# LayerNorm sums of a convolution branch: one ones-product per sum in chunks 1 to 3

## The chip, the cores and the metric

One core of one Trainium2 chip. The metric is the device time of one execution in microseconds; shown is the median of three runs.

## The reference

One layer of a streaming encoder for 2048 prompt frames and 64 sample frames. The convolution branch is the part that matters here: 512 channels, `u = a * sigmoid(gate)`, a causal depthwise convolution of width 31 plus a bias, then a LayerNorm over the 512 channels of each frame, swish, and a 512 x 512 projection `w_pw`.

```python
def _layernorm(x, g, b):
    mu = jnp.mean(xf, axis=-1, keepdims=True)
    xc = xf - mu
    y = xc * lax.rsqrt(jnp.mean(xc * xc, axis=-1, keepdims=True) + EPS)
    return y * g + b
...
c = _causal_dwconv(u_ext, w_dw) + b_dw
c = silu(_layernorm(c, g_cn, b_cn)) @ w_pw
```

The other branch is a stick-breaking attention of 8 heads. Both go through `w_out`, and a feed-forward layer (4096 wide, squared ReLU) follows.

## The kernel before

The frames are taken in four chunks of 512 (`NC = 4`); the last chunk carries the 64 sample frames as well. Every chunk passes through: gated projection (`ag`), k, v and q (`kvq`), convolution, LayerNorm, `pw`, attention, `out`, and the feed-forward layer. A product with a weight is made of three products of high and low parts (`mm3`: lines 2282 to 2284).

The order is written by hand, in slots. `window(c)` runs the feed-forward layer of chunk c in slots on every engine and, inside the same slots, the LayerNorm, `pw` and attention of chunk n = c + 1. A round `e` has 16 slots in windows 0 to 2: positions 0 to 7 are halves of f1 products (group j ends in the odd position 2j + 1), positions 8 to 15 are f2 products; a slot is twelve matrix products. After an f1 group ScalarE does ReLU, square and the high part (lines 1699, 1701, 1710), then VectorE writes `hid_lo` (line 2199). After an f2 product VectorE adds to `resid` (line 2189). In a slot each engine goes through its list in a fixed order: on VectorE weight splits (line 1787), convolution taps, the LayerNorm's step, `pw`'s low part, attention, f2's adds, `hid_lo`; on TensorE the LayerNorm's step, `pw`, then the slot's twelve products, then attention.

The LayerNorm of chunk c begins at slot `ln0(c)` of the window: 22, 18 and 14 for chunks 1, 2 and 3. The channels lie on partitions in four blocks (`CB = 4`) of 128, so a sum over channels is a product with a matrix of ones. Before the change, `ln` went by steps, one per slot:

- step 0, TensorE: four ones-products into one PSUM bank, the sum over channels (line 2440)
- step 1, VectorE: subtracts the mean from the four blocks (line 1979); ScalarE: their squares into `csq` (line 1520)
- step 2, TensorE: four ones-products over `csq` (line 2447)
- step 3, VectorE: variance (line 1983); ScalarE: Ln and Exp (lines 1523, 1525)
- step 4 on: VectorE refines the inverse root (lines 1986 to 1991) and scales, ScalarE and POOL make the sigmoid and the affine part, VectorE multiplies, `cT_hi` (ScalarE, line 1544) and `cT_lo` (VectorE, line 2007) follow, the last in step 11

Chunk 3 has a second piece of 64 columns (the sample), whose steps run 8 slots later. Chunk 0 has its LayerNorm in `front`.

`pw_slot(c)` is `ln0(c) + LN_STEPS` (8 more in chunk 3): 34, 30, 34. From there `pw`'s four products stand in four slots, each at the head of its slot; their results go out over ScalarE and VectorE (lines 1553, 2015) and SP (line 1058). Attention begins at `att_first(c) = pw_slot(c) + 4 + 1` and ends at slot 116; its steps are spread evenly over the slots between.

The weights pass through a ring of eight slabs in the order of `weight_order`; SP loads slab n when slab n - 8 is freed (`load_slab`, lines 844 to 865). `pw`'s two slabs have their place in that order by `pw_slot`:

```python
for e in range(FFE):
    w += [("f1", c, 4 * e + j) for j in range(4)]
    if pw and e == pw_slot(c + 1) // 16:
        w += pw
    w += [("f2", c, 4 * e + j) for j in range(4)]
```

Of the kernel before, what the change touches and what calls it, by code (L numbers as in the profile page):

```python
# [7 lines left out]
ALU = mybir.AluOpType  # L8
# [9 lines left out]
CC, CW = 512, 31  # L18
CB = CC // P
# [5 lines left out]
NC = SEQ // CHUNK  # L25
# [22 lines left out]
def conv_pieces(c):  # L48
    return [(0, 0, CHUNK)] + ([(SMP, CHUNK, DEC)] if c == NC - 1 else [])
# [72 lines left out]
    return 8 + 2 * len(tiles(c))  # L122


LN_STEPS = 12

EARLY = 11
LATE = [20, 43, 36, 28]
# [6 lines left out]
def ln0(c):  # L135

    return (LATE[c] + 1) // 2


def pw_slot(c):  # L140

    return ln0(c) + LN_STEPS + (8 if c == NC - 1 else 0)


def pw_step(c):
# [184 lines left out]
def build(nc, x_prompt, x_sample, cache_k, cache_v, state_conv, g_mix, w_in, w_dw, b_dw, g_cn, b_cn, w_pw,  # L330
# [3 lines left out]
    with ctx:  # L334
# [29 lines left out]
        ones = place("ones", [P, P])  # L364
# [32 lines left out]
        for c in range(2):  # L397
            n = TMAX if c else CHUNK
# [99 lines left out]
        def sem(name):  # L498
            return ctx.enter_context(nc.semaphore(name))
# [18 lines left out]
        kq_st = [sem(f"kq_st{i}") for i in range(2)]  # L518
        vp_out = [sem(f"vp_out{i}") for i in range(2)]
        sd_ok, id_ok = sem("sd_ok"), sem("id_ok")  # L520
        mean_ps, xc_ok, sq_ok, var_ps, var_ok, lnr_ok, yn_ok, sg_ok, cm_ok, c_hi, c_lo, cvo_ps, cvo_ok, cvo_out = (
            sem(n) for n in ("mean_ps", "xc_ok", "sq_ok", "var_ps", "var_ok", "lnr_ok", "yn_ok", "sg_ok", "cm_ok",
                             "c_hi", "c_lo", "cvo_ps", "cvo_ok", "cvo_out"))
        pw_ps, pw_hi, pw_lo, out_ps, out_add = (sem(n) for n in ("pw_ps", "pw_hi", "pw_lo", "out_ps", "out_add"))
        pw_st = [sem(f"pw_st{i}") for i in range(2)]
# [285 lines left out]

        def ln_step(c, slot):

            return [(n, slot - ln0(c) - 8 * n) for n in range(len(conv_pieces(c))) if 0 <= slot - ln0(c) - 8 * n < LN_STEPS]

        block = ctx.enter_context(nc.Block())

# [386 lines left out]
        def _(pool):  # L1204
# [40 lines left out]
            def ln(c, n, step):  # L1245
                a, q0, w = conv_pieces(c)[n]
                lb = c + n
                k = step - 5
                if 0 <= k < CB:
                    pool.wait_ge(yn_ok, CB * lb + k + 1)  # L1250
                    if CB * lb + k >= 2:
                        pool.wait_ge(cm_ok, CB * lb + k - 1)
                    nc.gpsimd.tensor_scalar(cid[:, k % 2, 0:w], conv_sum(c, k, a, w), vecs[:, k, CW + 1:CW + 2],
                                            vecs[:, k, CW + 2:CW + 3], ALU.mult, ALU.add).then_inc(id_ok, 1)
# [87 lines left out]
        def _(act):  # L1342
# [168 lines left out]
            def ln(c, n, step):  # L1511
                a, q0, w = conv_pieces(c)[n]
                lb = c + n
                nt = len(tiles(c))
                if step == 1:
                    if n:
                        act.wait_ge(yn_ok, CB * lb)
                    for k in range(CB):
                        act.wait_ge(xc_ok, CB * lb + k + 1)
                        nc.scalar.activation(csq[:, k, 0:w], conv_sum(c, k, a, w), ACT.Square).then_inc(sq_ok, 1)  # L1520
                if step == 3:
                    act.wait_ge(var_ok, lb + 1)
                    nc.scalar.activation(lnr[:, 0:w], lnv[:, 0:w], ACT.Ln).then_inc(sd_ok, 1)
                    act.wait_ge(sd_ok, 2 * lb + 1)
                    nc.scalar.activation(lnr[:, 0:w], lnr[:, 0:w], ACT.Exp, scale=-0.5).then_inc(sd_ok, 1)
                    nc.scalar.activation(unused[:], ident[:, 0:1], ACT.Sigmoid)
                k = step - 5
                if 0 <= k < CB:
                    act.wait_ge(yn_ok, CB * lb + k + 1)
                    if CB * lb + k >= 2:  # L1530
                        act.wait_ge(cm_ok, CB * lb + k - 1)
                    nc.scalar.activation(csig[:, k % 2, 0:w], conv_sum(c, k, a, w), ACT.Sigmoid,
                                         bias=vecs[:, k, CW + 2:CW + 3], scale=vecs[:, k, CW + 1:CW + 2]).then_inc(sg_ok, 1)
                if step == 7 and n == 0:
                    for m in (2 * nt - 2, 2 * nt - 1):
                        act.wait_ge(kq_st[m % 2], kq_stores(c, m))
                    for i in (nt - 2, nt - 1):
                        act.wait_ge(*value_stored(c, i))
                    act.wait_ge(vo_out[0], 16 * (2 * c + (nt + 1) // 2))
                    act.wait_ge(vo_out[1], 16 * (2 * c + 2))  # L1540
                k = step - 7
                if 0 <= k < CB:
                    act.wait_ge(cm_ok, CB * lb + k + 1)
                    nc.scalar.copy(cT_hi[:, k, a:a + w], conv_sum(c, k, a, w)).then_inc(c_hi, 1)
# [235 lines left out]
        def _(dve):  # L1780
# [192 lines left out]
            def ln(c, n, step):  # L1973
                a, q0, w = conv_pieces(c)[n]
                lb = c + n
                if step == 1:
                    dve.wait_ge(mean_ps, lb + 1)
                    for k in range(CB):
                        nc.vector.scalar_tensor_tensor(out=conv_sum(c, k, a, w), in0=ps[:, Z_BANK, 0:w], scalar=-1.0 / CC,
                                                       in1=conv_sum(c, k, a, w), op0=ALU.mult, op1=ALU.add).then_inc(xc_ok, 1)  # L1980
                if step == 3:
                    dve.wait_ge(var_ps, lb + 1)
                    nc.vector.tensor_scalar(lnv[:, 0:w], ps[:, Z_BANK + 1, 0:w], 1.0 / CC, EPS, ALU.mult, ALU.add).then_inc(var_ok, 1)
                if step == 4:
                    dve.wait_ge(sd_ok, 2 * lb + 2)
                    nc.vector.scalar_tensor_tensor(out=ntmp[:, 0:w], in0=lnr[:, 0:w], scalar=-0.5, in1=lnr[:, 0:w],
                                                   op0=ALU.mult, op1=ALU.mult).then_inc(lnr_ok, 1)
                    dve.wait_ge(lnr_ok, 3 * lb + 1)
                    nc.vector.tensor_tensor(ntmp[:, 0:w], ntmp[:, 0:w], lnv[:, 0:w], ALU.mult).then_inc(lnr_ok, 1)
                    dve.wait_ge(lnr_ok, 3 * lb + 2)  # L1990
                    nc.vector.scalar_tensor_tensor(out=lnr[:, 0:w], in0=ntmp[:, 0:w], scalar=1.5, in1=lnr[:, 0:w],
                                                   op0=ALU.add, op1=ALU.mult).then_inc(lnr_ok, 1)
                    dve.wait_ge(lnr_ok, 3 * lb + 3)
                    dve.wait_ge(xc_ok, CB * (lb + 1))
                for k in {4: (0,), 5: (1, 2), 6: (3,)}.get(step, ()):
                    nc.vector.tensor_tensor(conv_sum(c, k, a, w), conv_sum(c, k, a, w), lnr[:, 0:w],
                                            ALU.mult).then_inc(yn_ok, 1)
                k = step - 6
                if 0 <= k < CB:
                    dve.wait_ge(sg_ok, CB * lb + k + 1)  # L2000
                    dve.wait_ge(id_ok, CB * lb + k + 1)
                    nc.vector.tensor_tensor(conv_sum(c, k, a, w), csig[:, k % 2, 0:w], cid[:, k % 2, 0:w],
                                            ALU.mult).then_inc(cm_ok, 1)
                k = step - 8
                if 0 <= k < CB:
                    dve.wait_ge(c_hi, CB * lb + k + 1)
                    nc.vector.tensor_tensor(conv_low(c, k, a, w), conv_sum(c, k, a, w),
                                            cT_hi[:, k, a:a + w].bitcast(F32), ALU.subtract).then_inc(c_lo, 1)
# [271 lines left out]
        def _(pe):  # L2280
# [151 lines left out]
            def ln(c, n, step):  # L2432
                a, q0, w = conv_pieces(c)[n]
                lb = c + n
                if step == 0:
                    if n:
                        pe.wait_ge(xc_ok, CB * lb)
                    for k in range(CB):
                        pe.wait_ge(taps, TAPS * c + taps_in_order[c].index((k, CW - 1)) + 1)
                        ins = nc.tensor.matmul(ps[:, Z_BANK, 0:w], ones[:], conv_sum(c, k, a, w), start=k == 0, stop=k == CB - 1)  # L2440
                    ins.then_inc(mean_ps, 1)
                if step == 2:
                    if n:
# [312 lines left out]
```

## Time and profile before

| | before |
|---|---|
| median of 3 runs | 2761.16 us (2758.79 to 2766.84) |
| profiled execution | 2764.65 us, its span 2762.8 us |
| TensorE, weight loads of TensorE | 96%, 81% of the span |
| VectorE, ScalarE, POOL | 65%, 41%, 21% |
| mean granted clock of TensorE | 0.989 of full speed |

A busy share is an average over the whole span. What a step costs has to be read in its own stretch: from the timeline of each engine there, in which a bracket at the end of a row gives the idle time before the instruction and the one that ended it.

### The profile page before, as it was taken

The numbers are of one execution on the slowest core, as the hardware profiler recorded it, in microseconds if no ns is written. First come the engines' busy times: TensorE is split into PE (matmuls) and PEld (weight loads), VectorE is DVE, ScalarE is ACT, GpSimd is POOL, SyncE is SP. The second block draws the span as 40 slices with busy tenths as digits, with TensorE's granted clock in tenths as the row PEclk, the third lists the DMA queues.
The fourth block names the chain that finished last, engine by engine and source line by source line (L and its number), as shares of the span: only waits on it lengthen the run. The fifth ranks groups of instructions, "written<-read, shape, count | busy, mean of one in ns | idle before, by whom it ended". The sixth has DMA issues, their size and how long they took to land. (4 is left out here: it accounts for less than half of the span.)

```text
span 2762.8 us, 37728 instructions
## 1 busy us (share of the span) xinstructions
PE 2665.8 (96%) x13832; PEld 2248.4 (81%) x13832; DVE 1782.7 (65%) x2776; ACT 1123.7 (41%) x2221; POOL 580.8 (21%) x523
## 2 busy tenths in 40 slices
PE   7988899999999999999999999999999999999999
PEld 6757778788887888788888797778888887889998
DVE  6996777577762577367775358736888851755444
ACT  4334524455552122355554212334666630333342
POOL 2122210022210010032231002102333310434230
PEclk9999999999999999999999999999999999999999
DMA  9796797697669568465554746854455447355452
GB/s 325 254 342 205 234 353 276 254 332 264 254 219 370 220 220 288 168 232 181 182 179 156 308 183 220 266 203 148 151 191 174 163 160 293 122 187 179 167 198 96
DMA packets 294754, 616.21 MB, mean 223 GB/s; under 512 B 23665, under 2 KB 188529, under 8 KB 250029
## 3 DMA queue, kind: packets, MB, share of 16 engines
q1 hardware_dynamic: 294573, 613.80, 62.7%
q8 instruction: 113, 1.85, 0.3%
q14 instruction: 68, 0.56, 0.1%
HBM read 444.79 MB, written 168.94 MB: 222 GB/s over the span
## 5 line engine op out<-in xcount | busy, mean ns | idle before, releaser
L1265 POOL TENSOR_TENSOR beta<-beta,stay 128x512 f32<-128x512 f32 (+3 forms) x328 | 312.4, 953 | 890.1 <-DVE stay L2035 854.1
L2282 PE MATMUL ps<-h2T_hi,w_s 128*128 128x512 f32 (+2 forms) x976 | 370.7, 380 | 8.4 <-DMA w_s<-w_scratch 4.4
L2284 PE MATMUL ps<-h2T_hi,w_s 128*128 128x512 f32 (+2 forms) x976 | 359.2, 368 | 0.0
L2283 PE MATMUL ps<-h2T_lo,w_s 128*128 128x512 f32 (+2 forms) x976 | 358.9, 368 | 0.0
L1569 ACT ACTIVATE stay<-ps 128x512 f32<-128x512 f32 (+3 forms) x328 | 174.7, 533 | 346.5 <-PE ps L2483 223.8
L2550 PE MATMUL ps<-w_s,hid_hi 128*128 128x512 f32 x768 | 308.3, 401 | 0.0
L2551 PE MATMUL ps<-w_s,hid_lo 128*128 128x512 f32 x768 | 299.9, 390 | 0.0
L2552 PE MATMUL ps<-w_s,hid_hi 128*128 128x512 f32 x768 | 299.8, 390 | 0.0
L2189 DVE TENSOR_TENSOR resid<-ps,resid 128x512 f32<-128x512 f32 x256 | 174.0, 686 | 192.5 <-PE ps L2552 191.8
L2035 DVE TENSOR_TENSOR_SCAN stay<-stay,stay,ones 128x512 f32<-128x512 f32 x192 | 274.3, 1429 | 0.0
L1827 DVE SCALAR_TENSOR_TENSOR cacc<-uT,vecs,cacc 128x512 f32<-128x512 f32 (+1 forms) x360 | 259.6, 776 | 1.5
L2199 DVE TENSOR_TENSOR hid_lo<-ps,hid_hi 128x512 fp32r<-128x512 f32 x96 | 66.2, 690 | 261.9 <-ACT hid_hi L1710 261.9
L2282 PEld LDWEIGHTS ps<-h2T_hi,w_s 128*128 128x128 f32 x976 | 185.2, 190 | 38.4 <-DMA w_s<-w_scratch 4.5
L2284 PEld LDWEIGHTS ps<-h2T_hi,w_s 128*128 128x128 f32 x976 | 184.8, 189 | 30.9
L2283 PEld LDWEIGHTS ps<-h2T_lo,w_s 128*128 128x128 f32 x976 | 185.4, 190 | 26.3 <-issue 1.0
L2045 DVE TENSOR_TENSOR aT_lo<-ps,aT_hi 128x512 fp32r<-128x512 f32 (+3 forms) x328 | 189.5, 578 | 14.6 <-ACT aT_hi L1581 8.6
L2483 PE MATMUL ps<-a_k,a_q 128*128 128x512 f32 (+3 forms) x640 | 186.7, 370 | 8.8 <-DMA a_k<-k_scratch 8.3
L1581 ACT CAST aT_hi<-ps 128x512 fp32r<-128x512 f32 (+3 forms) x328 | 174.3, 531 | 19.3 <-PE ps L2493 14.7
L2493 PE MATMUL ps<-ident,beta 128*128 128x128 f32 (+1 forms) x1104 | 174.9, 273 | 7.2 <-DVE aT_lo L2045 7.0
L1570 ACT ACTIVATE beta<-ps 128x512 f32<-128x512 f32 (+3 forms) x328 | 173.7, 530 | 0.0
L2552 PEld LDWEIGHTS ps<-w_s,hid_hi 128*128 128x128 f32 x768 | 144.2, 188 | 31.9
L2550 PEld LDWEIGHTS ps<-w_s,hid_hi 128*128 128x128 f32 x768 | 144.4, 188 | 28.5 <-DVE resid L2189 0.4
(267 smaller groups left out, 5840.7 us busy)
## 6 DMA issues: line engine op xcount, KB each, us to landing
w_s<-w_scratch SPq DMA_DIRECT2D x254, 1024.0 KB, 8.3
w_scratch<-w_s SPq DMA_DIRECT2D x94, 1024.0 KB, 8.6
w_raw<-in_w_ff SPq DMA_DIRECT2D x92, 512.0 KB, 5.6
a_k<-k_scratch SPq DMA_DIRECT2D x80, 256.0 KB, 3.8
a_v<-v_scratch SPq DMA_DIRECT2D x80, 256.0 KB, 4.1
a_q<-q_scratch SPq DMA_DIRECT2D x64, 256.0 KB, 4.7
w_s<-w_scratch SPq DMA_DIRECT2D x28, 512.0 KB, 6.5
w_raw<-in_w_in SPq DMA_DIRECT2D x20, 512.0 KB, 7.9
```

Source lines behind the costliest of these rows:

```text
L1265: nc.gpsimd.tensor_tensor(v[0:q.r, 0:n], v[0:q.r, 0:n], stay_of(q.z)[0:q.r, 1:n + 1], ALU.mult).then_inc(s_a, 1)
L1827: nc.vector.scalar_tensor_tensor(out=acc, in0=uT[:, k, tap:tap + wd], scalar=vecs[:, k, tap:tap + 1], in1=acc, op0=ALU.mult, op1=ALU.add). ...
L2035: nc.vector.tensor_tensor_scan(v[0:q.r, 0:q.n][:, ::-1], v[0:q.r, 0:q.n][:, ::-1], ones[0:q.r, 0:1].to_broadcast([q.r, q.n]), init, ALU.mu ...
L2045: ins = nc.vector.tensor_tensor(aT_lo[:, o, 0:full, q.t * P:q.t * P + q.r], bank[:, 0:full * q.r].rearrange("p (a b) -> p a b", a=full), a ...
L2282: nc.tensor.matmul(out, w[0], x[0], start=start, stop=False)
L2283: nc.tensor.matmul(out, w[0], x[1], start=False, stop=False)
L2284: return nc.tensor.matmul(out, w[1], x[0], start=False, stop=stop)
L2483: ins = nc.tensor.matmul(ps[0:q.r, Z_BANK + q.z % 2, 0:q.n], x, a_k[:, k0:k0 + q.n], start=v == 0, stop=v == 1)
L2493: ins = nc.tensor.transpose(ps[0:w, T_BANK + q.z % 2, b * q.r:(b + 1) * q.r], beta[q.z % 4][0:q.r, b * P:b * P + w], ident[0:q.r, 0:q.r])
L2550: nc.tensor.matmul(o, hid_hi[x][:, k, q0:q0 + r], wh[:, c0:c0 + BANK], start=k == 0, stop=False)
L2551: nc.tensor.matmul(o, hid_lo[x][:, k, q0:q0 + r], wh[:, c0:c0 + BANK], start=False, stop=False)
L2552: ins = nc.tensor.matmul(o, hid_hi[x][:, k, q0:q0 + r], wl[:, c0:c0 + BANK], start=False, stop=k == 3)
```

## The change

In chunks 1 to 3, VectorE adds the four blocks up to one before each sum (two adds, then one that waits for both), and TensorE makes one ones-product of the result. The adds take a step each: step 0 the fold of the sums, step 1 the product, step 2 the subtractions and squares, step 3 the fold of the squares, step 4 the product; everything after it comes two steps later. So the LayerNorm has 14 steps in these chunks, not 12, and `pw_slot` is 36, 32, 36; `att_first` moves with it. `csq` holds the folds. Chunk 0 stays as it is. ScalarE's, POOL's and the later VectorE steps are the same with `later = 2` added to their step.

```diff
-LN_STEPS = 12
+def ln_steps(c):
+    return 14 if c else 12
...
-    return ln0(c) + LN_STEPS + (8 if c == NC - 1 else 0)
+    return ln0(c) + ln_steps(c) + (8 if c == NC - 1 else 0)
...
             def ln(c, n, step):
                 a, q0, w = conv_pieces(c)[n]
                 lb = c + n
-                if step == 1:
+                later = 2 if c else 0
+                if c and step == 0:
+                    if c == 1:
+                        dve.wait_ge(out_ps, 8)
+                    dve.wait_ge(kvq_ps, 12 * c + 3 * len(tiles(c)))
+                    if n:
+                        dve.wait_ge(yn_ok, CB * lb)
+                    for h in range(2):
+                        for k in (2 * h, 2 * h + 1):
+                            dve.wait_ge(taps, TAPS * c + taps_in_order[c].index((k, CW - 1)) + 1)
+                        nc.vector.tensor_tensor(csq[:, h, 0:w], conv_sum(c, 2 * h, a, w), conv_sum(c, 2 * h + 1, a, w),
+                                                ALU.add).then_inc(folded, 1)
+                    dve.wait_ge(folded, 6 * (lb - 1) + 2)
+                    nc.vector.tensor_tensor(csq[:, 0, 0:w], csq[:, 0, 0:w], csq[:, 1, 0:w], ALU.add).then_inc(folded, 1)
+                if c and step == 3:
+                    for h in range(2):
+                        dve.wait_ge(sq_ok, CB * lb + 2 * h + 2)
+                        nc.vector.tensor_tensor(csq[:, 2 * h, 0:w], csq[:, 2 * h, 0:w], csq[:, 2 * h + 1, 0:w],
+                                                ALU.add).then_inc(folded, 1)
+                    dve.wait_ge(folded, 6 * (lb - 1) + 5)
+                    nc.vector.tensor_tensor(csq[:, 0, 0:w], csq[:, 0, 0:w], csq[:, 2, 0:w], ALU.add).then_inc(folded, 1)
+                if step == (2 if c else 1):
                     dve.wait_ge(mean_ps, lb + 1)
...
-                if step == 0:
+                if c and step == 1:
                     if n:
                         pe.wait_ge(xc_ok, CB * lb)
+                    pe.wait_ge(folded, 6 * (lb - 1) + 3)
+                    nc.tensor.matmul(ps[:, Z_BANK, 0:w], ones[:], csq[:, 0, 0:w], start=True, stop=True).then_inc(mean_ps, 1)
+                if c and step == 4:
+                    if n:
+                        pe.wait_ge(var_ok, lb)
+                    pe.wait_ge(folded, 6 * (lb - 1) + 6)
+                    nc.tensor.matmul(ps[:, Z_BANK + 1, 0:w], ones[:], csq[:, 0, 0:w], start=True, stop=True).then_inc(var_ps, 1)
+                if c == 0 and step == 0:
...
```

## Rows read from the trace of the kernel before

**Rows 1.** The page, first part: busy time, share of the span, instructions.

```profile
PE 2665.8 (96%) x13832; PEld 2248.4 (81%) x13832; DVE 1782.7 (65%) x2776; ACT 1123.7 (41%) x2221; POOL 580.8 (21%) x523
```

**Rows 2.** Waits of TensorE, whole span: waited for, total us, times, longest.

```profile
PE ps L2282 <- DMA w_s<-w_scratch: 5.5, 3, 4.4
```

**Rows 3.** Timeline of TensorE, chunks 1 and 3: start, us, instruction, idle before.

```profile
484.26 1.02 PE L2440 MATMUL ps<-cacc_second,ones 128*128 128x512 f32 x2
486.87 2.84 PE L2440 MATMUL ps<-cacc_second,ones 128*128 128x512 f32 x6 [1.58 <-DVE cacc_second L1827]
489.15 0.80 PE L2282 MATMUL ps<-h2T_hi,w_s 128*128 128x512 f32 x1
...
495.02 3.60 PE L2447 MATMUL ps<-csq,ones 128*128 128x512 f32 x8
498.05 0.79 PE L2550 MATMUL ps<-w_s,hid_hi 128*128 128x512 f32 x1
498.68 0.39 PE L2551 MATMUL ps<-w_s,hid_lo 128*128 128x512 f32 x1
...
1810.06 1.00 PE L2440 MATMUL ps<-cacc,ones 128*128 128x64 f32 x8
1810.87 0.47 PE L2282 MATMUL ps<-h2T_hi,w_s 128*128 128x512 f32 x1
```

**Rows 4.** Timeline of VectorE, chunk 1's LayerNorm.

```profile
488.06 0.68 DVE L2199 TENSOR_TENSOR hid_lo<-ps,hid_hi 128x512 fp32r<-128x512 f32 x1
488.66 1.21 DVE L1787 TENSOR_TENSOR w_s<-w_raw,w_s 128x1024 fp32r<-128x1024 f32 x1
489.80 2.47 DVE L1979 SCALAR_TENSOR_TENSOR cacc_second<-ps,cacc_second 128x512 f32<-128x512 f32 x4
497.06 0.69 DVE L2199 TENSOR_TENSOR hid_lo<-ps,hid_hi 128x512 fp32r<-128x512 f32 x1 [4.79 <-ACT hid_hi L1710]
...
505.88 0.68 DVE L1986 SCALAR_TENSOR_TENSOR ntmp<-lnr 128x512 f32<-128x512 f32 x1
506.60 0.69 DVE L1989 TENSOR_TENSOR ntmp<-ntmp,lnv 128x512 f32<-128x512 f32 x1
```

**Rows 5.** Timeline of ScalarE, chunk 1's squares and chunk 3's `cvout`.

```profile
490.51 2.43 ACT L1520 ACTIVATE csq<-cacc_second 128x512 f32<-128x512 f32 x4 [3.29 <-DVE cacc_second L1979]
...
1804.52 1.04 ACT L1682 COPY cvout<-ps 30x512 f32<-30x512 f32 x2
```

**Rows 6.** Timelines of TensorE and VectorE, chunks 2 and 3.

```profile
1096.22 3.60 PE L2440 MATMUL ps<-cacc,ones 128*128 128x512 f32 x8
...
1098.26 0.69 DVE L2199 TENSOR_TENSOR hid_lo<-ps,hid_hi 128x512 fp32r<-128x512 f32 x1 [3.58 <-ACT hid_hi L1710]
...
1780.60 0.69 DVE L2189 TENSOR_TENSOR resid<-ps,resid 128x512 f32<-128x512 f32 x1 [0.39 <-PE ps L2552]
...
1812.36 0.69 DVE L2199 TENSOR_TENSOR hid_lo<-ps,hid_hi 128x512 fp32r<-128x512 f32 x1 [2.56 <-ACT hid_hi L1710]
```

**Rows 7.** Timeline of TensorE: waits for weight slabs, chunks 2 and 3.

```profile
1168.89 0.80 PE L2282 MATMUL ps<-h2T_hi,w_s 128*128 128x512 f32 x1 [4.38 <-DMA w_s<-w_scratch]
1174.08 0.40 PE L2483 MATMUL ps<-a_k,a_q 128*128 128x256 f32 x2
...
1839.15 0.39 PE L2282 MATMUL ps<-h2T_hi,w_s 128*128 128x512 f32 x1
...
1846.67 0.47 PE L2282 MATMUL ps<-cT_hi,w_s 128*128 128x512 f32 x1 [0.54 <-DMA w_s<-w_scratch]
```

**Rows 8.** TensorE's timeline, and stretches: length, busy by engine, granted clock, DMA.

```profile
178.22 1.13 PE L2440 MATMUL ps<-cacc,ones 128*128 128x512 f32 x2 [1.90 <-DVE cacc L1827]
178.00:181.00 3.00, 2.78 (x10) 1.99 (x11) 2.62 (x6) 0.81 (x2) 0.00 (x0) 1.00 1.08 282
...
1862.42 0.50 PE L2282 MATMUL ps<-cT_hi,w_s 128*128 128x512 f32 x1 [3.23 <-DVE pwo L2015]
1863.00:1867.00 4.00, 4.00 (x13) 3.13 (x12) 0.00 (x0) 0.00 (x0) 0.00 (x0) 0.57 0.49 180
```

More of the change, by code:

```diff
@@ L520, in build @@
         sd_ok, id_ok = sem("sd_ok"), sem("id_ok")
-        mean_ps, xc_ok, sq_ok, var_ps, var_ok, lnr_ok, yn_ok, sg_ok, cm_ok, c_hi, c_lo, cvo_ps, cvo_ok, cvo_out = (
-            sem(n) for n in ("mean_ps", "xc_ok", "sq_ok", "var_ps", "var_ok", "lnr_ok", "yn_ok", "sg_ok", "cm_ok",
+        folded, mean_ps, xc_ok, sq_ok, var_ps, var_ok, lnr_ok, yn_ok, sg_ok, cm_ok, c_hi, c_lo, cvo_ps, cvo_ok, cvo_out = (
+            sem(n) for n in ("folded", "mean_ps", "xc_ok", "sq_ok", "var_ps", "var_ok", "lnr_ok", "yn_ok", "sg_ok", "cm_ok",
                              "c_hi", "c_lo", "cvo_ps", "cvo_ok", "cvo_out"))
@@ L812, in ln_step @@
         def ln_step(c, slot):
-            return [(n, slot - ln0(c) - 8 * n) for n in range(len(conv_pieces(c))) if 0 <= slot - ln0(c) - 8 * n < LN_STEPS]
+            return [(n, slot - ln0(c) - 8 * n) for n in range(len(conv_pieces(c))) if 0 <= slot - ln0(c) - 8 * n < ln_steps(c)]
         block = ctx.enter_context(nc.Block())
@@ L1247, in ln @@
                 lb = c + n
-                k = step - 5
+                k = step - 5 - (2 if c else 0)
                 if 0 <= k < CB:
@@ L1520, in ln @@
                         nc.scalar.activation(csq[:, k, 0:w], conv_sum(c, k, a, w), ACT.Square).then_inc(sq_ok, 1)
-                if step == 3:
+                if step == 3 + later:
                     act.wait_ge(var_ok, lb + 1)
@@ L1526, in ln @@
                     nc.scalar.activation(unused[:], ident[:, 0:1], ACT.Sigmoid)
-                k = step - 5
+                k = step - 5 - later
                 if 0 <= k < CB:
@@ L1533, in ln @@
                                          bias=vecs[:, k, CW + 2:CW + 3], scale=vecs[:, k, CW + 1:CW + 2]).then_inc(sg_ok, 1)
-                if step == 7 and n == 0:
+                if step == 7 + later and n == 0:
                     for m in (2 * nt - 2, 2 * nt - 1):
@@ L1540, in ln @@
                     act.wait_ge(vo_out[1], 16 * (2 * c + 2))
-                k = step - 7
+                k = step - 7 - later
                 if 0 <= k < CB:
@@ L1975, in ln @@
                 lb = c + n
-                if step == 1:
+                later = 2 if c else 0
+                if c and step == 0:
[18 more added lines that the diff above has]
+                    nc.vector.tensor_tensor(csq[:, 0, 0:w], csq[:, 0, 0:w], csq[:, 2, 0:w], ALU.add).then_inc(folded, 1)
+                if step == (2 if c else 1):
                     dve.wait_ge(mean_ps, lb + 1)
@@ L1980, in ln @@
                                                        in1=conv_sum(c, k, a, w), op0=ALU.mult, op1=ALU.add).then_inc(xc_ok, 1)
-                if step == 3:
+                if step == 3 + later:
                     dve.wait_ge(var_ps, lb + 1)
                     nc.vector.tensor_scalar(lnv[:, 0:w], ps[:, Z_BANK + 1, 0:w], 1.0 / CC, EPS, ALU.mult, ALU.add).then_inc(var_ok, 1)
-                if step == 4:
+                if step == 4 + later:
                     dve.wait_ge(sd_ok, 2 * lb + 2)
@@ L1994, in ln @@
                     dve.wait_ge(xc_ok, CB * (lb + 1))
-                for k in {4: (0,), 5: (1, 2), 6: (3,)}.get(step, ()):
+                for k in {4: (0,), 5: (1, 2), 6: (3,)}.get(step - later, ()):
                     nc.vector.tensor_tensor(conv_sum(c, k, a, w), conv_sum(c, k, a, w), lnr[:, 0:w],
                                             ALU.mult).then_inc(yn_ok, 1)
-                k = step - 6
+                k = step - 6 - later
                 if 0 <= k < CB:
@@ L2003, in ln @@
                                             ALU.mult).then_inc(cm_ok, 1)
-                k = step - 8
+                k = step - 8 - later
                 if 0 <= k < CB:
@@ L2441, in ln @@
                     ins.then_inc(mean_ps, 1)
-                if step == 2:
-                    if n:
-                        pe.wait_ge(var_ok, lb)
+                if c == 0 and step == 2:
                     for k in range(CB):
```

## The prediction

> **What bounds the kernel now.** I read the page first, then the waits of TensorE, then its timeline around the ones-products of chunks 1 to 3, then VectorE and ScalarE in the same stretches, and last the granted clock. TensorE is busy for 96% of the span [rows 1]: what it no longer does, or no longer waits for, counts in full, and so does a new wait. Around the change a window slot is twelve products; 24 products run from 489.15 to 495.02 [rows 3], so with 0.40 for the slow first one a product takes 0.228 us and a slot 2.74. VectorE and ScalarE follow one slot behind, with slack that differs from slot to slot: after the second half of an f1 product, VectorE must wait for three ScalarE passes before it can write `hid_lo`. The product that ended at 495.02 [rows 3] got its `hid_lo` at 497.06 [rows 4]: 2.05 us, and VectorE is free at 2.65. That distance decides this case.
>
> **What is removed.** A ones-product appears as two passes. The four of chunk 1's variance hold TensorE from 495.02; the next product starts at 498.05, the one after it at 498.68 instead of 498.28 [rows 3]. So eight passes cost 3.43 us and six of them 2.57. Six sums of 512 columns (a mean and a variance in each of three chunks): 15.4. The 64-column sums of chunk 3's second piece cost 0.81 for eight passes (1810.06 to 1810.87) [rows 3], so six cost 0.6; two sums: 1.2. Chunk 1's wait of 1.58 for the last taps [rows 3] goes: 1.6. TensorE waits three times for a weight slab from the scratch, 5.5 in all with a longest of 4.4 [rows 2]. The two short ones (1.1 together) are chunk 1's and 3's first `pw` products; their slabs now have two more slots to land. The long one stands in chunk 2 at 1168.89 [rows 7]: f1 slabs 10 and 11 take ring places that `pw` frees. There `pw_slot` goes from 30 to 32, `feed_forward_order` divides it by 16, and so chunk 2's `pw` slabs move from e = 1 to e = 2 and those f1 slabs no longer stand behind them. That gives 4.38, and the half-speed stretch after it: twelve products took 5.19 (1168.89 to 1174.08 [rows 7]) instead of 2.74, thus 2.45. Together 6.8. Removed: 15.4 + 1.2 + 1.6 + 1.1 + 6.8 = 26.1.
>
> **What is added on VectorE.** A fold is two independent adds and one that waits for them. Independent operations of 512 columns follow each other at 0.60 (four in 2.47), dependent ones at 0.72 (505.88 to 506.60) [rows 4]; a fold takes 2.0 and reaches TensorE 0.1 later. VectorE's 65% [rows 1] does not make it free: each fold has its place in the queue.
>
> Chunk 1, mean. Without the products TensorE ends slot 22 at 484.26 + 2.74 = 487.0 [rows 3]. VectorE writes slot 21's `hid_lo` at 488.06 and a weight split until 489.87 [rows 4]; the fold is ready at 491.9. Wait 4.9.
> Chunk 1, variance. Let E be the end of slot 23, an f1 half: `hid_lo` done for the queue at E + 2.65, a split 1.15, four subtractions 2.47, the last square 0.67 after them (ScalarE ends at 492.94 [rows 5], VectorE at 492.27 [rows 4]), then one add and the dependent one: ready at E + 8.5. TensorE arrives two slots after E, at 5.5. Wait 3.0. Before, the subtractions fell behind slot 22, which has no `hid_lo`: moving them by one slot is what loses the slack.
> Chunk 2, mean. TensorE would end slot 18 at 1096.22 + 2.74 = 1098.96; `hid_lo` of slot 17 starts at 1098.26 [rows 6], so the fold is ready at 1101.0: wait 2.0. Variance: as in chunk 1 but no split, E + 7.45 against 5.46: wait 2.0.
> Chunk 3, first piece. Slots 13 and 15 end in f2 adds, which need no ScalarE: the add at 1780.60 [rows 6] starts right behind slot 13's product, 0.6 later the fold can start, and 0.6 + 2.0 + 0.1 = 2.7 is just the length of the slot that TensorE has to do. The same holds one step on for the variance. I take 0.1 for each.
> Chunk 3, second piece, mean. TensorE is now early: it began slot 22 at 1810.06 [rows 3], less 4.9 (two sums saved, 0.2 waited), and with 2.74 for the slot it reaches slot 23 at 1807.9. The fold stands behind slot 21's `hid_lo`, which was at 1812.36 [rows 6]. That moves up less, to about 1808.9: the root now sits at slot 19, where ScalarE also has the copies of `cvout` (1.04 [rows 5]) ahead of the gate of that slot, and the first sigmoid ahead of that of slot 21. Two more 512-column operations and a small fold follow: 0.6 + 0.6 + 0.6 for what is queued and 0.6 for the fold with its latency, ready at 1811.3, wait 3.4. Variance, from E as above: 2.65, four operations of 512 columns 2.4, four small subtractions 0.6 and the small fold with its latency 0.65 make E + 6.3 against 5.5: wait 0.8.
> Waits in all: 4.9 + 3.0 + 2.0 + 2.0 + 0.2 + 3.4 + 0.8 = 16.3.
>
> **The clock.** The granted clock falls after some waits. After 3.23 us at 1862.42 it is 0.57 on average over 4 us, a mix of its full level (2.4 GHz) and its half (1.2); after 1.90 at 178.22 it stays at 1.00 [rows 8]. At 0.57 for 4 us the toll is 4 x 0.43 = 1.7. I charge it for 4.9, 3.0 and 3.4, not for the two waits of 2.0, which lie nearer to 1.90: 5.1. The bounds: 0 (none falls) and 5 x 2.45 = 12.3 (all five fall, at the toll of rows 7). The Trainium skill, page "TensorE: Matmul & The Clock Gate", Part 1, states that the number of products run cold varies from run to run with the phase of the monitor; the two tolls seen here, 1.7 and 2.45, fit, and by it the sum would keep its middle and only spread.
>
> **What moves.** Chunk 2's `pw` slabs now go into places that f2 of e = 1 frees at the end of slot 31, and the first `pw` product stands at the head of slot 32, with no slot between. Nothing else is in SP's queue before them in that slot. In chunk 3 the same slabs are released at 1839.15, and the second is there at 1846.67 [rows 7]: 7.5. TensorE can do six products (1.37) as soon as the first lands, so 6.1 is lost, plus a clock toll that lies partly under the second transfer: 0.9. Together 7.0. Bounds: 6.1 (no toll) and 8.6 (6.1 + 2.45).
> The rest of the LayerNorm (Ln, Exp, POOL's scale-and-shift, sigmoids, `cT_lo`) moves two slots together with `pw`, so the number of slots between its last step and `pw` stays, and the first `pw` product has no wait for `cT_lo` to take over. SP's stores of `pwo` move with it and the attention's loads a little. Attention starts two slots later and ends at the same slot 116: chunk 3's 154 steps fall into 75 slots, not 77, so four slots get three steps. TensorE does the same work; I take 0, with 2 us as the upper bound (a wait of about 0.5 in each of the four). If `pwo`'s wait of 3.23 in chunk 3 [rows 8] goes with the later start, that is a gain of up to 4.9; it hangs on slot parity, which stays, so 0. SP, POOL and ScalarE issue the same number of instructions; VectorE gets 24 more, under its waits for TensorE elsewhere.
>
> **Sum.** 16.3 + 5.1 + 7.0 - 26.1 = +2.3. The profiled execution took 2764.65, 3.5 above the median of the three runs; against the median: 2761.16 + 2.3 = 2763.5.
>
> **The rivals.**
> A, the folds come in time. If VectorE runs ahead of where I put it, the 16.3 of waits and their 5.1 of clock go: 2763.5 - 21.4 = 2742.1. For it: VectorE is idle for 35% of the span [rows 1]. Against it: the `hid_lo` rows stand directly ahead of the fold's place in chunks 1 and 2, and ScalarE's three passes cannot be shortened. A half of it, with chunk 1's split out of the way and chunk 3's second piece in time, saves about half of that: some 2752. Chance 0.13.
> B, the clock, on the other side. Place: behind the five waits of 2.0 and more, and behind chunk 2's slab wait. Price: 2.45 each, not 1.7 thrice, is 12.3 - 5.1 = 7.2, and 1.6 more at the slabs: 2763.5 + 8.8 = 2772.3. It decides once these six stretches cost 2.0 each, 12.0 instead of the 6.0 charged. For it: [rows 7]; against it: [rows 8], the clock held after 1.90 us. Chance 0.15.
>
> **How the numbers follow.** About 0.3% (8.3 us) is what a measurement of this kernel can tell from no change. The forecast with its bounds (clock 0 to 12.3, slabs 6.1 to 8.6, attention 0 to 2, each seldom at its end) gives 2756 to 2770; its chance is 0.72. The range reaches to A's half and most of the way to B: 2752 to 2771. Faster by over 0.3% is A (0.13), slower is B (0.15), within is the forecast (0.72).
>
> **What would show it.** In the profile of the changed kernel each 512-column sum is one product of two passes. The waits of TensorE should name the folds on VectorE, the longest of some 5 us in chunk 1, 2 and 2 in chunk 2, and about 3.4 in chunk 3's second piece; the clock should be below 1.0 after the long ones. In chunk 2 there should be a wait of 5 to 6 us for the slabs of `pw` at the head of slot 32, and none at slot 36. I am wrong if the folds show no waits (A), if `pw` in chunk 2 starts at once, or if attention takes visibly longer.

## The result and the profile after

| | before | after |
|---|---|---|
| median, 5 runs of each on one chip | 2761.16 us (2758.79 to 2767.27) | 2773.43 us (2769.49 to 2778.66) |
| ratio with 95% interval | | 1.0044 [1.0034, 1.0055] |
| profiled execution, its span | 2764.65, 2762.8 us | 2773.43, 2771.6 us |

The change makes the kernel slower by 12.3 us. The forecast was 2763.5, with a range of 2752 to 2771. Between the two profiled executions the difference is 8.8, because the one of before lay 3.5 above its median; the stages below add up to those 8.8.

First line of the page, after: busy time, share of the span and instructions. It answers to [rows 1].

```profile
PE 2658.5 (96%) x13784; PEld 2243.4 (81%) x13784; DVE 1802.6 (65%) x2800; ACT 1122.0 (40%) x2221; POOL 590.7 (21%) x523
```

TensorE has 48 instructions fewer and is busy 7.3 us less; VectorE has the 24 more that were counted. With less to do and a span 8.8 longer, TensorE must stand still for some 16 us more. The waits of TensorE over the whole span, after (engine, line, waited for: us in total, times, longest):

```profile
PE ps L2522 <- DVE aT_lo L2068: 16.3, 23, 2.3
...
PE ps L2462 <- DVE csq L1991: 9.7, 3, 4.7
...
PE ps L2467 <- DVE csq L1998: 5.2, 3, 2.8
PE ps L2305 <- DMA w_s<-w_scratch: 4.9, 1, 4.9
```

The two `csq` lines are the folds and the `w_scratch` line is the slab wait; both were forecast. The top line is the attention, and it was not: in before the same wait is

```profile
PE ps L2493 <- DVE aT_lo L2045: 7.0, 16, 0.9
```

The folds one by one, in TensorE's timeline after (start, us, instruction, idle time before it); they answer to [rows 3], the `pw` rows to [rows 7, 8]:

```profile
489.75 2.08 PE L2462 MATMUL ps<-csq,ones 128*128 128x512 f32 x2 [4.72 <-DVE csq L1991]
...
503.49 2.07 PE L2467 MATMUL ps<-csq,ones 128*128 128x512 f32 x2 [2.83 <-DVE csq L1998]
...
1098.41 1.12 PE L2462 MATMUL ps<-csq,ones 128*128 128x512 f32 x2 [1.83 <-DVE csq L1991]
...
1109.43 1.12 PE L2467 MATMUL ps<-csq,ones 128*128 128x512 f32 x2 [1.69 <-DVE csq L1998]
...
1142.66 0.77 PE L2305 MATMUL ps<-cT_hi,w_s 128*128 128x512 f32 x1 [4.88 <-DMA w_s<-w_scratch]
...
1812.88 0.41 PE L2462 MATMUL ps<-csq,ones 128*128 128x64 f32 x2 [3.12 <-DVE csq L1991]
...
1823.86 0.41 PE L2467 MATMUL ps<-csq,ones 128*128 128x64 f32 x2 [0.72 <-DVE csq L1998]
...
1868.46 0.69 PE L2305 MATMUL ps<-cT_hi,w_s 128*128 128x512 f32 x1 [3.22 <-DVE pwo L2038]
```

Each sum is one product of two passes. The first wait is long for the reason given ahead of the run, as VectorE's timeline after shows; its fold is the last two rows:

```profile
485.96 0.68 DVE L2222 TENSOR_TENSOR hid_lo<-ps,hid_hi 128x512 fp32r<-128x512 f32 x1
486.56 1.21 DVE L1789 TENSOR_TENSOR w_s<-w_raw,w_s 128x1024 fp32r<-128x1024 f32 x1
487.69 1.28 DVE L1988 TENSOR_TENSOR csq<-cacc_second,cacc_second 128x512 f32<-128x512 f32 x2
489.01 0.69 DVE L1991 TENSOR_TENSOR csq<-csq 128x512 f32<-128x512 f32 x1
```

VectorE is never idle here: `hid_lo` and a weight split of 1.21 stand ahead of the fold while TensorE waits. The clock behind these waits (stretch, its length, busy by engine, granted clock, DMA share, GB/s), answering to [rows 8]:

```profile
490.00:494.00 4.00, 4.00 (x10) 2.50 (x11) 0.00 (x0) 0.00 (x0) 0.00 (x0) 0.62 1.03 368
503.50:507.50 4.00, 4.00 (x9) 2.54 (x10) 2.27 (x3) 2.32 (x2) 0.00 (x0) 0.60 1.03 425
1098.40:1101.40 3.00, 2.99 (x11) 2.17 (x12) 0.00 (x0) 0.00 (x0) 0.00 (x0) 1.00 1.02 429
1109.40:1112.40 3.00, 2.97 (x11) 2.16 (x12) 1.38 (x2) 2.60 (x4) 0.00 (x0) 1.00 1.06 376
1142.60:1146.60 4.00, 3.94 (x9) 3.04 (x10) 0.00 (x0) 0.00 (x0) 0.00 (x0) 0.50 1.01 426
1813.00:1817.00 4.00, 4.00 (x13) 3.19 (x14) 0.76 (x1) 0.62 (x2) 0.99 (x2) 0.62 0.01 2
```

In this execution it falls behind the waits of 4.72, 2.83, 4.88 and 3.12 and stays at 1.00 behind those of 1.83 and 1.69. The last section shows that the 1.83 does not always leave it there.

**Where the 8.8 us are.** TensorE's timeline was cut in both profiles at the first `out` product, the first `kvq` product, the first `pw` product and the first score of each chunk. The LayerNorm's stage has two more slots in it after the change and the attention's two fewer; they are taken out at 2.74 each (5.48). The forecast's terms are put beside them:

| stage | forecast | measured |
|---|---|---|
| chunk 1, up to `pw` | +4.6 | +2.9 |
| chunk 1, `pw` | -0.6 | -1.6 |
| chunk 1, attention | 0 | -2.7 |
| chunk 2, up to `pw`, without the slab wait | -1.1 | -1.0 |
| chunk 2, slab wait and `pw` | +7.0 | +4.9 + 2.7 |
| chunk 2, attention: the old slab wait and its toll | -6.8 | -6.8 |
| chunk 2, the rest of the attention | 0 | +3.1 |
| chunk 3, up to `pw` | -0.2 | -0.4 |
| chunk 3, `pw` | -0.6 | -0.8 |
| chunk 3, attention | 0 | +8.3 |
| everything else | 0 | +0.2 |
| sum | +2.3 | +8.8 |

(In chunk 2's attention only the sum of its two lines, -3.7, is measured; the old wait and its toll are [rows 7].) One line is far off: chunk 3's attention. To see it in the profile, take three rounds of 16 slots each, cut where VectorE writes the `hid_lo` of slots 49, 65, 81 and 97. Before:

```profile
1936.20:2022.70 86.50, 85.24 (x494) 72.74 (x493) 73.71 (x116) 55.36 (x117) 32.19 (x32) 1.00 0.50 163
2022.70:2109.20 86.50, 85.28 (x494) 72.79 (x493) 73.71 (x116) 55.43 (x118) 32.19 (x32) 1.00 0.50 167
2109.20:2195.80 86.60, 85.34 (x494) 72.85 (x493) 73.75 (x117) 55.46 (x118) 32.20 (x32) 1.00 0.49 160
```

After:

```profile
1930.70:2020.43 89.73, 87.49 (x508) 74.38 (x507) 75.02 (x119) 56.11 (x120) 32.70 (x33) 1.00 0.48 157
2020.43:2111.56 91.13, 86.64 (x500) 73.56 (x500) 76.27 (x118) 56.26 (x120) 35.84 (x33) 1.00 0.47 156
2111.56:2198.42 86.86, 85.87 (x493) 72.41 (x491) 74.92 (x116) 55.09 (x117) 32.27 (x32) 1.00 0.48 164
```

Before, every round is the same 86.5. After, the first two last 89.7 and 91.1 and the third is back at 86.9, all at a full clock. The first two hold 33 steps of attention and not 32, which is about (86.5 - 16 x 2.74)/32 = 1.3 us of the difference in each, moved there from elsewhere; the rest is lost. In the second, TensorE is idle for 91.13 - 86.64 = 4.5, against 1.2 before.

What differs between the rounds is how the steps are dealt. Before, 154 steps fall on 77 slots, 39 to 115: each slot has steps 2i and 2i + 1, an even pair. After, 75 slots share them, and three steps fall in slots 59, 78, 97 and 115. Behind a slot with three, the pairs are shifted: slots 60 to 77 and 98 to 114 hold the second step of one old pair and the first of the next, an odd pair, and slots 79 to 96 hold even pairs again. The second round above is mostly odd (12 of its 16 slots), and its 4.5 of waits stand in the odd slots 68, 70 and 72; the third is nearly all even. From 1884 to 2318, before:

```profile
PE ps L2493 <- DVE aT_lo L2045: 5.1, 12, 0.6
```

and after, the same stretch:

```profile
PE ps L2522 <- DVE aT_lo L2068: 11.5, 14, 2.3
```

So the profile names 6.4 of the 8.3. Counted by slot, TensorE's waits in chunk 3's attention after, all causes together, are 6.7 in the 35 odd slots, 2.8 in the four with three steps (2.33 of it in slot 97) and 2.3 in the 36 even ones; before, the 77 even slots have 5.8.

### The profile page after: what moved, and what is told of

It is laid out like the page before. It is cut to its first block and busy times, and to the rows that moved or that the text cites. A ratio compares the mean times of both kernels' runs of the same rounds, so it can differ in the third digit from the quotient of the medians.

```text
span 2771.6 us, 37664 instructions
## 1 busy us (share of the span) xinstructions
PE 2658.5 (96%) x13784; PEld 2243.4 (81%) x13784; DVE 1802.6 (65%) x2800; ACT 1122.0 (40%) x2221; POOL 590.7 (21%) x523
## 3 DMA queue, kind: packets, MB, share of 16 engines
q8 instruction: 113, 1.85, 0.3%
## 5 line engine op out<-in xcount | busy, mean ns | idle before, releaser
L2522 PE MATMUL ps<-ident,beta 128*128 128x128 f32 (+1 forms) x1104 | 175.1, 274 | 16.7 <-DVE aT_lo L2068 16.3
L2522 PEld LDWEIGHTS ps<-ident,beta 128*128 128x128 f32 (+1 forms) x1104 | 132.7, 140 | 54.2 <-issue 28.4
L2581 PEld LDWEIGHTS ps<-w_s,hid_hi 128*128 128x128 f32 x768 | 144.4, 188 | 31.8
```

The source lines that it names most:

```text
L2522: ins = nc.tensor.transpose(ps[0:w, T_BANK + q.z % 2, b * q.r:(b + 1) * q.r], beta[q.z % 4][0:q.r, b * P:b * P + w], ident[0:q.r, 0:q.r])
L2581: ins = nc.tensor.matmul(o, hid_hi[x][:, k, q0:q0 + r], wl[:, c0:c0 + BANK], start=False, stop=k == 3)
```

## The experiments

All ratios are against the kernel before, run beside it on the same chip; "after" is the changed kernel of the section above. Three questions were open: whether the attention's loss comes from its later start, what the folds and the slab stall are worth alone, and then whether the three-step slots or the shifted pairs cost the time.

**1. The attention ends two slots later (e1).** The changed kernel, attention ending at slot 118 in chunks 1 to 3, so that it has as many slots as before again (77 in chunks 1 and 3, 81 in chunk 2).

```diff
-    return 58 if c == 0 else 116
+    return 58 if c == 0 else 118
```

> The changed kernel (2773.4), with the attention of chunks 1 to 3 ending at slot 118, not 116, so that it has as many slots as before the change: chunk 3 has two steps in each of 77 slots again. Theory 1, the attention's denser steps cost the time: in chunk 3 the stretch from the first score to the output projection is 426.5 us, against 423.7 less two slots of 2.74 before, so 8.3 too long, with 11.5 us of waits for aT_lo against 5.1; in chunk 2 some 3 us. Both go: 2762 to 2765, the waits for aT_lo in chunk 3 back at about 5. Rival, the loss is in the LayerNorm's folds and the clock after them (and the attention only shows it): within 2 us of 2773.

Measured: 2772.24, ratio 1.0046 [1.0033, 1.0058]: no gain in all, as the rival had it. But the stages of the theory moved as it said: chunk 3's attention took 8.9 less than after, chunk 2's 3.1 less. Chunk 1's took 9.5 more, and TensorE's timeline there has a wait that neither kernel had:

```profile
805.12 0.79 PE L2512 MATMUL ps<-a_k,a_q 128*128 128x512 f32 x1 [5.36 <-DMA a_k<-k_scratch]
```

Chunk 1's slots decide when loads of `a_k` can start. The expectation missed that, and experiment 5 leaves chunk 1 alone.

**2. The kernel before, with the later start alone (e2).**

```diff
-    return pw_slot(c) + pw_step(c) * CB + 1
+    return pw_slot(c) + pw_step(c) * CB + (3 if c else 1)
```

> The kernel before (2761.2) with nothing of the change but the later start of attention: two slots later in chunks 1 to 3, the end stays at slot 116. No fold, 12 steps, slabs as before. Theory 1 (denser steps): 2769 to 2773, slower by 8 to 11, with waits for aT_lo of 2 us in chunk 3. Rival (folds and clock): within 2 us of 2761.

Measured: 2768.81, ratio 1.0028 [1.0016, 1.0039]. No fold, no moved slab, and a loss of about 7. From 1884 to 2318 its wait is that of after, to the digit:

```profile
PE ps L2493 <- DVE aT_lo L2045: 11.5, 14, 2.3
```

The later start with the old end is enough to make this loss. Chunk 3's attention is 429.46 long here, 2.9 more than after with the same waits, because the clock fell behind two of them (1.85 and 2.33) that left it at full in the profiled execution after.

**3. Chunk 2's `pw` slabs earlier (e3).** The changed kernel, with these slabs put between f2 of e = 1 and f1 of e = 2.

```diff
-        if pw and e == pw_slot(c + 1) // 16:
+        if pw and c != 1 and e == pw_slot(c + 1) // 16:
             w += pw
         w += [("f2", c, 4 * e + j) for j in range(4)]
+        if pw and c == 1 and e == 1:
+            w += pw
```

> The changed kernel (2773.4) with chunk 2's two pw slabs in another place of the weight order, between f2 of e = 1 and f1 of e = 2: they then take ring places that f1 of e = 1 frees, some twelve slots before their use. Theory 1: this removes the wait of 4.9 at the head of slot 32 and the half-speed stretch behind it (2.7), so 2765 to 2767, and leaves the waits for aT_lo in chunks 2 and 3 as they are. Rival, the slab wait hides work that VectorE has to do anyway: the wait moves to the pw results or the attention's first steps and less than 3 us is gained.

Measured: 2764.76, ratio 1.0012 [1.0003, 1.0020], 8.7 under after. The wait of 4.88 is gone; the stages up to `pw` and of `pw` are 5.0 and 2.7 shorter than after. So the stall cost 7.7, of which 2.7 lay behind the wait itself, not the 0.9 of the forecast.

**4. Both (e4).** Edits 1 and 3 together.

> Both edits, attention to slot 118 and chunk 2's slabs early. Theory 1, the two costs lie in different stretches and add up: 2773.4 - 9.5 - 7.6 = 2754 to 2758, faster than the kernel before. If the two overlap: no better than the better one alone.

Measured: 2765.05, ratio 1.0014 [1.0005, 1.0023]. A miss: chunk 1's attention lost 9.6 to `a_k`, as in e1, which cancels the gain elsewhere.

**5. The later end in chunks 2 and 3 only (g1).**

```diff
-    return 58 if c == 0 else 116
+    return 58 if c == 0 else 116 if c == 1 else 118
```

> The changed kernel (2773.4) with the attention of chunks 2 and 3 alone ending at slot 118; chunk 1's ends at 116 as in the changed kernel. Theory 1 in its second form: the first try took 8.9 us out of chunk 3's attention and 3.1 out of chunk 2's, and gave 9.5 back in chunk 1, where the shifted steps ran into a 5.4 us wait for a_k. Without chunk 1: 2760 to 2763. Rival (a fixed sum of time that shows up wherever the trace has room): again about 2772.

Measured: 2760.44, ratio 0.9997 [0.9989, 1.0006], 13.0 under after. Its wait from 1884 to 2318:

```profile
PE ps L2522 <- DVE aT_lo L2068: 5.6, 13, 0.7
```

That is before's again (5.1, 12, 0.6). By stage it gains 8.7 in chunk 3's attention and 3.1 in chunk 2's, 11.8 together.

**6. The changed order without the folds (g6).** Four ones-products per sum, in steps 1 and 4; everything else as after. The core of it, next to the folds' removal on VectorE:

```diff
-                if c and step == 1:
+                if step == (1 if c else 0):
...
-                if c == 0 and step == 2:
+                if step == (4 if c else 2):
```

> The changed kernel (2773.4) without the folds: the schedule with its 14 steps, pw and attention two slots later and the slab order stay, but TensorE makes four ones-products again in steps 1 and 4 and VectorE adds nothing up. Theory: the folds save 15.4 + 1.2 of products and cost 14.9 of waits and three stretches of slow clock, 4.6 by the granted clock after them, so the folds alone are worth nothing: 2768 to 2774, with the waits for csq gone and no low clock in chunk 1's LayerNorm. Rival 1, the folds are the loss: 2761. Rival 2, the folds gain what the removed products cost: 2785 to 2790.

Measured: 2765.43, ratio 1.0019 [1.0011, 1.0028], 8.0 under after. It was expected that the folds would be worth about nothing; they cost. How much is less sure: the profiled execution here is the fastest of its twelve, 3.5 below their median, and by the two ratios the difference is 6.9, give or take some 4. By stage, after against this kernel, the stretches that hold the folds give chunk 1 +5.7, chunk 2 -1.2 and chunk 3 -0.3, together 4.2. The `pw` stages give another +1.0 in chunk 2 and +1.6 in chunk 3, but those hold no fold: both kernels have the same waits there (4.9 and 3.2), and behind them the clock was 0.50 and 0.57 over 4 us after, 0.57 and 1.00 here. Chunk 1's thirty microseconds without folds (stretch, length, TensorE's busy time first, the granted clock third from the end):

```profile
480.00:510.00 30.00, 30.00 (x120) 22.09 (x119) 16.84 (x23) 13.55 (x18) 0.00 (x0) 1.00 0.94 345
```

and with them, after:

```profile
480.00:510.00 30.00, 22.45 (x81) 16.34 (x80) 19.24 (x26) 10.14 (x14) 0.00 (x0) 0.89 0.90 332
```

7.55 us of waits and a clock of 0.89, to save two sums of 2.57. In chunk 2, where the waits are short and the clock held in this execution, the folds win 1.2; where it fell behind the first of them, as in g1, the same stage is 1.7 longer and the gain is gone. This kernel also shows that chunk 1's tap wait of 1.58 [rows 3] went through the later slot, not through the fold.

**7. Edits 3 and 5 together (g2).**

> Chunk 2's slabs early and the attention of chunks 2 and 3 to slot 118. Theory: both gains in full, 2773.4 - 8.7 - 12 = 2752 to 2755, faster than the kernel before by 0.25 to 0.35%. If they overlap: 2760.

Measured: 2753.54, ratio 0.9973 [0.9962, 0.9984]: faster than before. The gain is 19.9 where 8.7 and 13.0 make 21.7: the two losses are separate and add up, within the noise.

**8. The LayerNorm of chunks 1 and 2 one slot later (g8).** On top of g2, so that a fold no longer stands right behind a `hid_lo`. Shown against the changed kernel, without edit 3.

```diff
-    return (LATE[c] + 1) // 2
+    return (LATE[c] + 1) // 2 + (1 if c in (1, 2) else 0)
...
-    return 58 if c == 0 else 116
+    return 58 if c == 0 else (116, 119, 118)[c - 1]
```

> The kernel just named, and the LayerNorm of chunks 1 and 2 begins one slot later (23 and 19), so that the folds and subtractions follow slots without hid_lo; chunk 2's attention ends at 119. Theory, the waits come from the slot parity: chunk 1's 4.7 falls to about 2, its 2.8 and chunk 2's 1.8 and 1.7 vanish, with the slow clock behind them; 8 us less than the kernel just named, 2744 to 2748. Rival, VectorE is simply late there: the waits stay within 1 us of what they were, 2752 to 2755.

Measured: 2745.41 (2743.34 to 2748.97), ratio 0.9947 [0.9935, 0.9958]: faster than both kernels, by 15.9 and 28. The folds' waits in TensorE's timeline:

```profile
486.33 1.88 PE L2464 MATMUL ps<-csq,ones 128*128 128x512 f32 x2 [2.01 <-DVE csq L1993]
...
498.40 1.13 PE L2469 MATMUL ps<-csq,ones 128*128 128x512 f32 x2 [1.13 <-DVE csq L2000]
...
1102.08 1.13 PE L2469 MATMUL ps<-csq,ones 128*128 128x512 f32 x2 [1.83 <-DVE csq L2000]
```

Chunk 1's went from 4.72 and 2.83 to 2.01 and 1.13, and chunk 2's first is gone. Chunk 2's second, expected to vanish, is 1.83 (1.69 after): one slot later it is this fold that stands right behind a `hid_lo`, in VectorE's timeline:

```profile
1099.41 0.69 DVE L2224 TENSOR_TENSOR hid_lo<-ps,hid_hi 128x512 fp32r<-128x512 f32 x1 [3.25 <-ACT hid_hi L1714]
1100.02 1.28 DVE L1997 TENSOR_TENSOR csq<-csq 128x512 f32<-128x512 f32 x2
```

Both the waits that went and the one that stayed fit the forecast's account, that a fold's price is its place in VectorE's queue behind `hid_lo`. That the folds pay in this kernel is not shown: no run has its deal and slabs without the folds, and g2's 2753.5 less what the folds cost (4 to 8 by g6) would be near the same time.

**9. The kernel before with odd pairs (h1).** Chunk 3's steps shifted by one: one step in slot 39, odd pairs in 40 to 115, the last step in 116. No slot has three steps. This and the next tell the two theories of the attention's loss apart.

```diff
-    if slot < a or slot >= b:
+    if slot < a or slot >= b + (c == NC - 1):
         return range(0)
+    if c == NC - 1:
+        return range(max(0, 2 * (slot - a) - 1), min(n, 2 * (slot - a) + 1))
```

> The kernel before (2761.3), where each slot of chunk 3's attention holds an even step and the next odd one; here all of chunk 3's steps move by one, so that slot 39 holds one step, slots 40 to 115 an odd step and the next even one, and slot 116 the last. No slot has three steps, and nothing else changes. Theory 2, the pairing: in the changed kernel slots 65 to 80, nearly all with odd pairs, took 91.1 us (33 steps) against 86.5 (32 steps) with even pairs; over 76 slots that is some 15 to 20 us, 2775 to 2781. Theory 1, the slots with three steps: 2760 to 2763.

Measured: 2774.26, ratio 1.0038 [1.0026, 1.0051], just under the expected 2775. Chunk 3's attention took 10.8 more than before. Its wait from 1884 to 2318:

```profile
PE ps L2495 <- DVE aT_lo L2047: 13.3, 20, 1.1
```

The theory of the three-step slots foretold no loss here. It falls as the whole cause: odd pairs lose time without any such slot.

**10. The changed kernel with even pairs (h2).** The same 75 slots; slots 78 and 115 take four steps, all the others one old pair.

```diff
+    if c == NC - 1:
+        return range(2 * (n // 2 * (slot - a) // (b - a)), 2 * (n // 2 * (slot - a + 1) // (b - a)))
```

> The changed kernel (2773.4), attention of chunk 3 still in slots 41 to 115, but its steps are dealt out in whole even pairs: two slots (78 and 115) hold four steps, all others two. Theory 2, the pairing: chunk 3's stretch falls from 426.5 to 418 to 420 us, in all 2765 to 2767. Theory 1, the slots with more than two steps: no better than 2771.

Measured: 2766.70, ratio 1.0015 [1.0006, 1.0024], 6.7 under after. Chunk 3's attention is 420.06 long against 426.52, and the wait from 1884 to 2318 falls back:

```profile
PE ps L2524 <- DVE aT_lo L2070: 5.6, 11, 1.2
```

Against before's 418.2 (423.67 less the two slots), 1.9 are left. That is what two fewer slots cost with the pairs kept (the two slots of four steps have 1.3 of waits). The other 6.5 of the 8.3 go with the odd pairs and the slots of three steps, which this edit takes out together.

**11. The kernel before with the earlier slabs (f1).** Edit 3 on before, where it should remove the wait of 4.38 [rows 7].

> The kernel before (2761.3) with nothing of the change but chunk 2's pw slabs in the other place (between f2 of e = 1 and f1 of e = 2), so that no f1 slab waits for the place that pw frees. Theory: the wait of 4.4 at slot 36 and the slow clock behind it (2.45) go, 2753 to 2756. Rival, the wait moves to the next slab: 2760 to 2762.

Measured: 2758.55, ratio 0.9986 [0.9977, 0.9995], half of what was expected. Chunk 2's attention lost its 6.9, but `pw` took 3.3 more, with a new wait in it:

```profile
1164.55 0.79 PE L2284 MATMUL ps<-h2T_hi,w_s 128*128 128x512 f32 x1 [2.44 <-DVE pwo L2017]
```

## Why the prediction was wrong

**What held.** The waits of TensorE for the folds were forecast as 4.9, 3.0, 2.0, 2.0, 3.4 and 0.8; they are 4.72, 2.83, 1.83, 1.69, 3.12 and 0.72. They came from reading VectorE's queue ahead of each fold. (The terms of chunk 2's second add up to E + 7.3, not 7.45, so to 1.8 and not 2.0.) The clock fell where it was charged and held behind the two short waits; that it held behind the 1.83 was luck, since it fell there in four of the seven profiled kernels that have this wait. Behind the long ones, 4 us at 0.62, 0.60 and 0.62 are tolls of 1.5, 1.6 and 1.5, against 1.7 each. The slab wait went from slot 36 to the head of slot 32. Rival A needed the folds in time; they were not. Rival B's time, 2772.3, is near the measured one, but its mechanism is not what happened: behind 1.83 and 1.69 the clock did not fall in the profiled execution.

**The step that failed** is the attention's in "What moves": "TensorE does the same work; I take 0, with 2 us as the upper bound (a wait of about 0.5 in each of the four)." The step saw that 154 steps fall in 75 slots and that four slots get three; it did not ask what the other 71 get. Thirty-five of them got odd pairs, and those hold the most: 6.7 of TensorE's waits, against 2.8 in the four slots. What two fewer slots cost by themselves is 1.9 (h2), inside that bound; the odd pairs and the three-step slots cost another 6.5 in chunk 3 (h2 against after), and odd pairs by themselves made before slower by 12 (h1). Chunk 2's attention was in the same sentence and lost 3.1. With 8.3 + 3.1 = 11.4 on the term, the forecast would have been 2775, near what came. Its last sign, "if attention takes visibly longer", is the one that showed.

**Terms that were off in size.** Behind chunk 2's slab wait the forecast had 0.9 and the stage shows 2.7; that the clock's fall is hidden under a second transfer was a guess, and it was not (4 us at 0.50 make 2.0 of it). The wait itself was 4.88, not 6.1, so that the term as a whole was 7.6 against 7.0. On the other side, chunk 1 came out 5.4 better than forecast (-1.4 for +4.0): 2.7 of it in its attention, where two waits for `a_k` (2.6 together in before) went with the later start, which the forecast had in "a little", and 2.7 before it. The folds as a whole are 16.3 + 5.1 - 16.6 = +4.8 by the forecast's own terms; their stages cost 4.2 (g6), and the medians 8.0. So the sign of that idea was visible ahead of the run: chunk 1's folds cost more than chunk 2's and 3's can win.

**What stays open.** Why an odd pair is dearer is only read from rows. VectorE's timeline after, ahead of the product at 2061.28 that waited 1.85 for the `aT_lo` in the last row:

```profile
2055.72 0.69 DVE L2222 TENSOR_TENSOR hid_lo<-ps,hid_hi 128x512 fp32r<-128x512 f32 x1 [2.26 <-ACT hid_hi L1712]
...
2056.39 1.28 DVE L2058 TENSOR_TENSOR_SCAN stay<-stay,stay,ones 128x512 f32<-128x512 f32 x1
2057.59 0.66 DVE L2068 TENSOR_TENSOR aT_lo<-ps,aT_hi 128x512 fp32r<-128x512 f32 x1
2058.28 0.89 DVE L2080 TENSOR_TENSOR ohl<-osb,ohl 64x256 fp32r<-64x256 f32 x1
...
2059.28 1.27 DVE L2058 TENSOR_TENSOR_SCAN stay<-stay,stay,ones 128x512 f32<-128x512 f32 x1
2060.47 0.67 DVE L2068 TENSOR_TENSOR aT_lo<-ps,aT_hi 128x512 fp32r<-128x512 f32 x1
```

VectorE waits 2.26 for `hid_lo`'s input and is then busy without a gap for two whole steps and the end of a head (`ohl`) before it reaches that `aT_lo`. It fits that an odd pair puts other VectorE work than an even one behind an f1 half's `hid_lo`, but no run moved one of these alone. Chunk 2's 3.1 went when its attention got 81 slots again (e1, g1); the pairs there were not tried by themselves. And in chunk 3 the price of the pairs was not parted from that of the three-step slots; TensorE waits 0.19 per odd slot after and 0.18 in h1, against 0.08 per even slot in before.

## What to carry to other kernels

When a stage that is dealt evenly over slots loses or gains a slot, write out the deal for every slot, not only the slots with an extra step: a shift by one step changes which work meets which in all slots behind it. What a fold that spares TensorE products costs hangs on its place in its producer's queue; read that queue slot by slot, and move the stage by a slot before dropping the idea (here from 1.0044 to 0.9947, with the deal and the slabs put right). After moving a stage, look also at the loads that its position releases (`a_k`, `pw`'s slabs): they gave or took 3 to 10 us here.

## What the runs showed of the hardware

The length of a wait alone does not tell whether the clock falls, and the same wait in the same place goes either way. The 1.83 ahead of chunk 2's first fold stands in seven of the profiled kernels. Behind it the clock stays at 1.00 over the next 4 us in three (after, e3, h2) and is 0.57 to 0.66, a mix of full (2.4 GHz) and half (1.2), in four (e1, e4, g1, g2). The attention's 2.33 in slot 97 leaves it at 1.00 after and at 0.60 in e2. The wait of 3.2 for `pwo` ahead of chunk 3's `pw` brings it down in twelve of the thirteen profiles, but not in g6's; the 2.01 in g8 brings it down. The 2.33 after and its stretch, then the stretches of e2 (2.33), g1 (1.83), g6 (3.23) and g8 (2.01), one profile each:

```profile
2201.10 0.41 PE L2522 MATMUL ps<-ident,beta 128*128 128x128 f32 x2 [2.33 <-DVE aT_lo L2068]
2201.00:2205.00 4.00, 3.90 (x22) 3.48 (x23) 4.00 (x6) 1.29 (x4) 1.70 (x2) 1.00 1.00 377
```

```profile
2193.70:2197.70 4.00, 3.98 (x16) 3.67 (x17) 4.00 (x5) 1.23 (x3) 1.60 (x2) 0.60 1.01 378
```

```profile
1099.00:1103.00 4.00, 4.00 (x10) 2.85 (x11) 0.00 (x0) 0.00 (x0) 0.00 (x0) 0.62 1.02 426
```

```profile
1858.40:1862.40 4.00, 4.00 (x23) 3.48 (x24) 0.38 (x2) 0.59 (x1) 0.00 (x0) 1.00 0.62 234
```

```profile
486.40:490.40 4.00, 4.00 (x9) 2.50 (x10) 3.78 (x6) 2.14 (x4) 0.00 (x0) 0.57 1.01 426
```

So a toll of some 1.4 to 2.0 us (4 us at 0.66 to 0.50) comes and goes behind the same wait from one profiled execution to the next, and a difference of that size between two profiled stages shows nothing by itself.

VectorE's scan of 512 columns takes 1.26 to 1.28 us where POOL does nothing beside it (28 of the 72 in the stretch of the three rounds after), but 1.74 in this one, where POOL multiplies a tile of the same size beside it. After, first VectorE, then POOL:

```profile
2061.11 1.74 DVE L2058 TENSOR_TENSOR_SCAN stay<-stay,stay,ones 128x512 f32<-128x512 f32 x1
```

```profile
2060.68 1.09 POOL L1266 TENSOR_TENSOR beta<-beta,stay 128x512 f32<-128x512 f32 x1 [1.79 <-DVE stay L2058]
```

The Trainium skill, page "GPSIMD Engine Reference", section "8. Key points", says that GpSimd shares its SBUF interfaces with VectorE and contends with VectorE instructions that have two SBUF inputs; the scan has two, and these rows agree, though no run took POOL's multiplication away. It does not explain the loss: the 72 scans of these rounds take 106.4 us before and 107.4 after.
